# Router logits from rows before the first norm, the output product by halves, and another order of the last expert and the last norm

## The reference, cut to what matters

```python
def _finish(x, nsa_o, hg_o, ga, gb, w_pa, w_pb, w_o, ln1_g, ln1_b, moe_w, ln2_g, ln2_b):
    mix = (sigmoid(ga) * (nsa_o @ w_pa) + sigmoid(gb) * (hg_o @ w_pb)) @ w_o
    h = _layernorm(DN_ALPHA * x + mix, ln1_g, ln1_b)
    return _layernorm(DN_ALPHA * h + _moe(h, *moe_w), ln2_g, ln2_b)

def _moe(x, w_router, b_router, w_gu, b_gu, w_dn, b_dn):
    logits = x @ w_router + b_router
    top_v, top_e = top_k(logits, 4); gate = softmax(top_v)
    # for each of the 32 experts e, over the rows that chose it:
    h = xb @ w_gu[e] + b_gu[e]
    gt = minimum(h[:, :D_FF], 7.0); up = clip(h[:, D_FF:], -7.0, 7.0)
    ys = ((up + 1.0) * (gt * sigmoid(1.702 * gt))) @ w_dn[e] + b_dn[e]
    # y = the sum over a row's four experts of gate * ys
```

## Time and profile before

| | |
|---|---|
| Time, median of 3 runs | 1409.96 us (1408.92 to 1412.66) |
| Profiled execution, time / span | 1412.07 us / 1410.4 us |
| TensorE busy | 1378.1 us, 98% of the span |
| VectorE, ScalarE, GpSimd busy | 436.0, 296.8, 93.2 us |
| DMA moved | 476.70 MB, 464.85 MB of it through SP's queue |
| TensorE's granted clock, mean | 0.993 of full |

### The profile page before, as it was taken

One profiled execution on the slowest core, in us unless ns is written; L12 is line 12 of the kernel. 1 busy time (PEld: TensorE's weight loads), 2 busy tenths in 40 slices (PEclk: granted clock), 3 DMA queues, 4 the chain that ended last, 5 costly groups with the idle time before them and its releaser, 6 DMA issues.

```text
span 1410.4 us, 20548 instructions
## 1 busy us (share of the span) xinstructions
PE 1378.1 (98%) x7829; PEld 656.6 (47%) x7829; DVE 436.0 (31%) x946; ACT 296.8 (21%) x507; POOL 93.2 (7%) x122
## 2 busy tenths in 40 slices
PE   9999999998999999999999999999999999999996
PEld 6667999766774433333333333333333333333332
DVE  0345774763335321122112211221113111221115
ACT  1125531342311311111111111111112111111111
POOL 0031400203000000000000000000000000000000
PEclk9999999999999999999999999999999999999998
DMA  8831350729784999999999999999999999999993
GB/s 293 285 106 57 109 165 23 211 80 293 210 310 197 404 372 425 428 428 426 428 429 428 428 428 428 428 428 429 428 428 429 428 428 428 428 429 429 427 430 129
DMA packets 77622, 476.70 MB, mean 338 GB/s; under 512 B 9506, under 2 KB 37474, under 8 KB 52674
## 3 DMA queue, kind: packets, MB, share of 16 engines
q1 hardware_dynamic: 73328, 464.85, 81.3%
q0 software_dynamic: 2288, 9.51, 2.0%
q10 hardware_dynamic: 1954, 1.63, 0.4%
HBM read 471.54 MB, written 8.59 MB: 340 GB/s over the span
## 4 chain that ended last, share of the span: by engine, by line
PE 86%; DMA 10%; DVE 2%; ACT 1%; issue 0%; SPq 0%
PE bank L1313 27%; PE bank L1346 14%; DMA big<-in_w_gu 9%; PE bank L1003 4%; PE bank L1277 4%; PE bank L1256 4%; PE bank L765 3%; PE bank L749 2%; PE bank L1172 2%; PE bank L820 2%; PE bank L822 2%; PE bank L828 2%; PE bank L1185 2%; PE bank L1249 2%; PE bank L1267 1%; PE bank L1335 1%
## 5 line engine op out<-in xcount | busy, mean ns | idle before, releaser
L1313 PE MATMUL bank<-big,gates 128*64 128x512 f32 x1536 | 338.4, 594 | 4.5 <-DMA big<-in_w_gu 4.2
L1313 PEld LDWEIGHTS bank<-big,gates 128*64 128x64 f32 x1536 | 107.2, 137 | 216.7 <-issue 204.2
L1346 PE MATMUL bank<-big,gates 128*64 128x512 f32 x768 | 171.4, 595 | 0.0
L2397 DVE TENSOR_SCALAR gates<-bank 128x512 f32<-128x512 f32 x32 | 22.1, 692 | 434.5 <-PE bank L1326 434.5
L1653 ACT ACTIVATE gates<-gates 128x512 f32<-128x512 f32 x32 | 20.1, 630 | 452.1 <-DVE gates L2397 452.1
L1346 PEld LDWEIGHTS bank<-big,gates 128*64 128x64 f32 x768 | 53.0, 137 | 114.1 <-issue 114.1
L1727 POOL TENSOR_TENSOR gates<-gates,nsaT 128x192 f32<-128x192 f32 x64 | 31.4, 511 | 983.3 <-PE bank L1356 860.4
L2420 DVE TENSOR_TENSOR work<-work,bank 128x512 f32<-128x512 f32 x128 | 82.1, 682 | 42.5 <-PE bank L1277 42.5
L2416 DVE TENSOR_TENSOR work<-work,bank 128x256 f32<-128x256 f32 x32 | 13.5, 421 | 202.2 <-PE bank L1280 202.2
L1277 PE MATMUL bank<-gates 64*128 64x512 f32 x260 | 73.4, 641 | 0.9 <-ACT gates L1663 0.9
L1661 ACT ACTIVATE gates<-bank 128x512 f32<-128x512 f32 x32 | 19.1, 597 | 258.4 <-PE bank L1280 258.4
(11 more groups left out here) (391 smaller groups left out, 1622.0 us busy)
## 6 DMA issues: line engine op xcount, KB each, us to landing
big<-in_w_gu SPq DMA_DIRECT2D x96, 2048.0 KB, 22.7
big<-in_w_dn SPq DMA_DIRECT2D x48, 2048.0 KB, 25.9
front_rows<-in_w_gu SPq DMA_DIRECT2D x16, 2048.0 KB, 23.3
front_cols<-in_w_gu SPq DMA_DIRECT2D x15, 2048.0 KB, 21.5
front_cols<-in_w_dn SPq DMA_DIRECT2D x8, 2048.0 KB, 26.1
front_rows<-in_w_dn SPq DMA_DIRECT2D x8, 2048.0 KB, 28.6
big<-in_w_in SPq DMA_DIRECT2D x5, 2048.0 KB, 8.6
big<-in_cache_cmp_kv SPq DMA_DIRECT2D x64, 128.0 KB, 2.6
```

What stands on the lines that cost most here:

```text
L1313: last = pe.matmul(psum[2 + n][half * CAP:(half + 1) * CAP, :], xe[:, k % 4, (k // 4) * CAP:(k // 4 + 1) * CAP], weights_gu(slot, k % 2, c ...
L1346: last = pe.matmul(psum[5][half * CAP:(half + 1) * CAP, :], act_T[:, k % 4, (k // 4) * CAP:(k // 4 + 1) * CAP], ring_dn[slot][:, k % 4, ha ...
```

## The change

It does this:

1. Gate weights 3 go to another place in `big`, in two loads, and wait for the recurrence's states as well. The window rows of pass 0 no longer wait for products 7 and 8: two wait for four gate products, two for six. PE waits for all four at key block 8. Gate weights 4 are loaded as before and gate weights 5 after the eighth product.
2. `w_o` is stored and loaded as two halves of 512 columns, and `out_product` runs in the order 0, 2, 1, 3 (both first halves, then both second halves).
3. PE turns r = alpha*x + mix instead of h. The router's weights are multiplied by the norm's gain once (DVE), and each row's logits are scaled by its reciprocal deviation and moved by a multiple of the weights' sums afterwards. For this PE turns the gain and shift (16x128) and sums the scaled weights over partitions by a product with ones. h itself is scaled and shifted in six halves that stand between and behind the selections; the gather of expert 0 waits for them.
4. The loads of the expert weights ahead of expert 0 are put in another order. The gates' softmax is moved behind the count of rounds, POOL waits for it, and ACT copies alpha*h earlier.
5. The last expert is written out apart (PE and ACT) without gather and transposes for a next one. Its `combine` 1 and 2 and the transposes of the gates stand among the products with `w_dn`.
6. At the end the sample rows stay in quarters: statistics per quarter are joined by two products with a matrix of 0.25. The order is tile 0, sample rows, tile 1. Of tiles 0 and 1 the second half of the columns is scaled by ACT, and DVE multiplies by the gain and adds the shift.

```diff
-            sp.wait_ge(fill_done, 4)
+            sp.wait_ge(state_step, HH * 4)
+            sp.wait_ge(fill_done, 3)
             load_gates(3)
             load_rows(sp, 0, 3, rows_loaded[0])
-            for b4 in range(4):
+            for b4 in (2, 3, 0, 1):
                 if b4 % 2 == 0:
-                    sp.wait_ge(fill_done, 6 + b4)
-                if b4 == 2:
-                    sp.wait_ge(win_loaded, 32)
+                    sp.wait_ge(fill_done, 6 - b4)
                 load_window(0, b4, win_loaded)
             sp.wait_ge(pv_done, len(ITS))
             load_gates(4)
+            sp.wait_ge(fill_done, 8)
             load_gates(5)
...
                     if n == 8:
-                        pe.wait_ge(win_loaded, 32)
-                    if n == 10:
                         pe.wait_ge(win_loaded, 64)
...
             out_product(0)
+            pe.wait_ge(route_made, 11)
+            pe.matmul(psum[0][:, 2 * NE:4 * NE], C("ones"), wr_part, start=True, stop=True).then_inc(route_sent, 1)
+            turn_r(0)
+            turn_r(1)
+            out_product(2)
+            router_part(0, 0)
+            router_part(0, 1)
+            turn_r(2)
             out_product(1)
-            turn_h(0)
-            out_product(2)
-            pe.wait_ge(params_loaded, 32)
-            router_product(0)
-            out_product(3)
-            turn_h(1)
+            turn_r(3)
+            router_part(1, 0)
+            pe.wait_ge(route_made, 12)
+            out_product(3, {4: (lambda: turn_r(4),), 6: (lambda: router_part(1, 1),)})
+            router_part(2, 0)
+            turn_r(5)
             keep_busy(1)
-            router_product(1)
-            turn_h(2)
-            keep_busy(1)
-            router_product(2)
+            router_part(2, 1)
             keep_busy(4)
...
-            keep_busy(3)
+            keep_busy(4)
...
                 for k in range(KD):
+                    if k == 2 and final:
+                        combine(i, 1)
+                    if k == 3 and final:
+                        pe.wait_ge(y_added, i * 5 + 9)
+                    if k == 4 and final:
+                        combine(i, 2)
+                        turn_gates(i)
...
+            apply_half(1, 0, 3)
+            apply_half(1, 1, 5)
+            residual(1, 1, 5)
+            norm_scale(1, 2)
             select_tile(1)
+            scale_logits(2)
             select_tile(2)
             dve.wait_ge(select_ready, 3)
+            apply_half(2, 0, 4)
...
+            end_scale(0, 0)
+            end_apply(0).then_inc(own.next("end_step"), 1)
+            end_second(0).then_inc(y_ready, 1)
...
+            end_apply(1).then_inc(y_ready, 1)
+            end_second(1).then_inc(y_ready, 1)
```

More of the change, by code:

```diff
@@ L260, in trunk_kernel @@
         w_pb = part(big, 4096, [HH, D])
-        w_o = part(big, 8192, [KD, D])
+        w_o = [part(big, 8192 + 4096 * half, [KD, 512]) for half in range(2)]
         front_cols = sb("front_cols", [P, KD * NT + 2 * HG * NT])
@@ L338, in trunk_kernel @@
         b_router = part(small, 554, [NE])
+        wr_part = part(small, 256, [2 * NE])
+        wr_sums = part(small, 320, [2 * NE])
+        gb = part(small, 384, [2 * KD])
+        gb_rows = part(small, 426, [P])
+        ln_move = part(small, 586, [3])
+        wr_b = part(work, 6144, [KD, NE])
         ln_parts = part(small, 640, [3, 2, 6])
@@ L352, in trunk_kernel @@
         ln2 = [part(big, D * n, [D]) for n in range(2)]
+        ln2_q = [part(big, 2 * D + D // 4 * n, [D // 4]) for n in range(2)]
+        mean_of = part(nsa_flat, 1024, [P])
+        ln_sum = part(small, 690, [4])
+        ln_shift = part(small, 694, [2])
         xg = part(xT, 0, [512])
@@ L1184, in out_product @@
+            pe.transpose(psum[0][:, 0:2 * KD], gb_rows[0:2 * KD, :], ident[0:2 * KD, 0:2 * KD]).then_inc(route_sent, 1)
+            def out_product(i, between={}):
                 for k in range(KD):
[L1185 removed]
+                    for work_ in between.get(k, ()):
+                        work_()
+                    last = pe.matmul(psum[(5 + i) % 8][:, :], mixT[:, k, (i // 2) * P:(i // 2 + 1) * P], w_o[i % 2][:, k, :],
@@ L1283, in combine, with turn_gates, expert @@
                 last.then_inc(comb_done, 1)
-            def expert(group, q):
+            def turn_gates(i):
+                pe.wait_ge(pg_ready, i + 1)
+                for t in range(3):
+                    last = pe.transpose(psum[0][:, t * P:(t + 1) * P], pg[:, t, :, :].rearrange("p a n -> p (a n)"), ident)
+                last.then_inc(pg_turned, 1)
+            def expert(group, q, final=False):
                 i = group * 4 + q
@@ L1330, in expert @@
                 combine(i, 0)
-                gather(i + 1)
+                if not final:
+                    gather(i + 1)
                 pe.wait_ge(act_ready, i + 2)
@@ L1350, in expert @@
                         last.then_inc(piece_free, 1)
-                combine(i, 2)
-                pe.wait_ge(pg_ready, i + 1)
-                pe.wait_ge(xg_copied, i + 2)
-                for t in range(3):
-                    last = pe.transpose(psum[0][:, t * P:(t + 1) * P], pg[:, t, :, :].rearrange("p a n -> p (a n)"), ident)
-                last.then_inc(pg_turned, 1)
+                if not final:
+                    combine(i, 2)
+                    pe.wait_ge(xg_copied, i + 2)
+                    turn_gates(i)
             gather_sample(0)
@@ new lines, in _ @@
+            dve.wait_ge(r_ready, 6)
+            for half in range(2):
+                norm_stats(h_rows, 2, half)
+            norm_scale(2, 0)
+            residual(0, 0, 2)
+            dve.wait_ge(route_sent, 4)
+            step(dve.tensor_copy(wr_sums, psum[0][:, 2 * NE:4 * NE]))
+            dve.tensor_tensor(wr_sums[:, NE:2 * NE], wr_sums[:, NE:2 * NE], b_router, ALU.add).then_inc(route_made, 1)
+            dve.wait_ge(route_made, 12)
+            scale_logits(0)
+            apply_half(0, 0, 1)
```

365 lines of the change are left out of this document (241 added, 124 removed).

## The result

| | before | after |
|---|---|---|
| Time, median (range) | 1409.88 us (1407.82 to 1412.66), 12 runs | 1411.32 us (1408.78 to 1413.93), 12 runs |
| Profiled execution, time / span | 1412.07 / 1410.4 us | 1411.22 / 1409.5 us |
| Ratio of times | | 1.0016, 95% interval 1.0009 to 1.0023 |

The change makes the kernel slower by 0.16%, about 2 us: within the 0.3% that the prediction counts as no change, but on the other side of it than the forecast of 1406.5 us, and just above its range of 1402.0 to 1411.0.

A forecast was written before the change was run, and what follows sets the result against it. The prediction took the end to hang on expert 0's start, through PE freeing ring places for weight loads. Terms -4.87, +0.6 and -0.2 gave -4.5 us; between 1407.6 and 1405.5 it took 1406.5 us, range 1402 to 1411.

The forecast's parts named there:

- part 1: Window rows and gate weights, pass 0: PE's 2.13 us wait and the half clock behind it go, -4.87 us.
- rival A: New PE gaps ahead of the count and in the last expert bring half clock, 1.7 us each: 1409.9 us; chance 0.21.
- What bounds the kernel: Experts: their end hangs on when PE frees ring places early on, so expert 0's start moves the end equally.
- nothing within the later experts does: Later experts: no change within them moves the experts' end; no time was reckoned there.
- part 3: Last expert: products with `w_dn` end later, less follows them, so the end's first product starts 1.2 us later.
- Rival B: Pass 1: the window's wait moves to POOL's selected rows, making the kernel slower, 1414.5 us; chance 0.07.
- Part 2: Router, up to expert 0: output product ends 4.5 us later, DVE's chain takes 7.2 us; +0.6 us in all.
- Part 4: The end: DVE's work from the last results to the last store shrinks by 1.4 us.
- C: Router, last expert and end: chains shorter than reckoned, -3 instead of +0.4 us, 1403.1 us; chance 0.22.
- D: Ahead of expert 0: its start doesn't move, as a weight piece or small load comes last; 1409.7 us; chance 0.05.

The follow-up runs named there:

- b1: The kernel before, unchanged, profiled again: 1408.77 us.
- e4: The changed kernel with the last expert back in the loop but the new end kept: 1406.78 us, ratio 0.9983 to before.
- e9: e4 with ACT's alpha*h copy earlier, router products of 128 columns for prompt rows only, and three more keep_busy products: 1405.37 us, ratio 0.9972 to before.
- e6: The changed kernel with four products nobody reads in PE's two gaps in the last expert: 1409.42 us, ratio 0.9999 to before.
- e2: The kernel before with only PE's last four experts written out behind the loop: 1410.18 us, ratio 1.0006.
- e5: e4 with PE's last four experts written out behind the loop, in the loop's own order: 1408.35 us, ratio 0.9996 to before.
- e3: The changed kernel with the last expert and the end as before: 1408.62 us, ratio 0.9993 to before.
- e1: The kernel before with only the gate-weight and window-row changes: 1409.33 us, ratio 0.9995.
- e8: e1 with router products of 128 columns instead of 32, for all rows: 1408.00 us, ratio 0.9991 to before.
- e10: e8 with the sample rows' router products of 32 columns again: 1406.57 us, ratio 0.9977 to before.
- b2: The kernel before, unchanged, profiled once more: 1408.66 us.

## Why the prediction was wrong, point by point

Start from b1, which is what ordinary faster executions of before look like, and go to the changed kernel's profile: G 0.15 earlier, G to O 1.8 less, O to E 2.5 more, E to L 1.0 more, L to end 0.9 more; together +2.5 us. The forecast had -4.87 for G to O, +0.6 for O to E, nothing for E to L and -0.2 for L to end, together -4.5. So the four stretches came out 3.1, 1.9, 1.0 and 1.1 us longer than forecast: the term of part 1 was more than twice too large, rival A's half clock came at both its places, and late code, which no rival had, lengthened the stream.

- **What bounds the kernel: right up to its last clause.** Places free up, loads leave and the hole ends 3.3 us earlier, as expert 0 does, and no experiment moved E to L by more than 0.5 us but the late code. That exception is what the last clause, "nothing within the later experts does", had ruled out (see part 3).
- **Part 1, -4.87 us: the wait went as forecast, the size was wrong, the largest error.** The step that failed is the 2.7 us of half clock in the sum, taken from one execution as if each had it. At full clock G to O shrinks by 1.8 us (b1 to after), which is about b1's wait of 1.94. The other 2.9 (G to O of the first profile less b1's) were the half clock of the one execution that was profiled. I had written that faster executions might have less of it, and took 1.0 us off the gain for it (1406.5 against 1405.5 us), too little. The page "TensorE: Matmul & The Clock Gate" of the Trainium skill (section "Why this matters for your kernels"), by whose bound the part was worth the wait only, came nearer the typical time, though its bound for a gap does not describe, where half clock does follow 2.13 us. Rival B didn't come: POOL's rows stayed without a wait.
- **Part 2, +0.6 us: near at full clock (b1 to e4: 47.70 to 48.56, +0.86), with luck, and +2.5 in the changed kernel's profile.** DVE's chain took 7.0 us against my 7.2, but the last output half is ready only 3.2 us later behind O and not 4.5, so that the count comes 0.6 us earlier behind O (40.24 to 39.62) where I had +0.1. From the count to expert 0 it is 1.5 us more (7.46 to 8.94), where I had 0.5 for `keep_busy`: there stands a wait that I did not see. DVE's start needs ACT's last copy, put behind two copies that wait for PE, and it costs PE 1.05 us (1.30 against 0.25 in e9). The two errors nearly cancel. The other 1.64 us in the changed kernel's profile are half clock behind the 2.03 us ahead of the count, which I had named in rival A and priced at 1.7.
- **Part 3, +1.2 us: the order right, the step incomplete.** At full clock (e6) `combine` starts 20.18 us behind L, before 19.08: +1.1. The changed kernel has 21.81, 1.6 more for half clock, the other half of rival A. What I had in no rival is the code: writing the last group out makes PE load it again while the chain hangs on the weights, +1.2 us in E to L of e2 (against the mean of before's three profiles) and +1.56 of e5 (against e4). The step that failed is "nothing within the later experts does": in E to L I had put the written-out code at nothing, and it took 1.0 to 1.6 us.
- **Part 4, -1.4 us: right, and a little small.** DVE's last stretch is 1.9 us shorter. L to end falls by 1.6 from e3 to e4, since 0.2 are given back by a product that now stands ahead of the first `combine`.
- **Rivals.** A is what the profile shows, at both its places and its prices; with 0.21 it was too low, for PE's gaps of 1.8 to 2.0 us were nearly as long as the one in rows 4. That it came ahead of the count in the execution profiled is partly chance, as e4's full clock behind the same gap shows. C, that everything is shorter, was too high. D did not come.

The Trainium skill ("Runtime: NRT & Kernel Launch", "Instruction fetch mechanics") says that code comes in 16 KiB blocks by a DMA queue of the engine's own, which agrees with the 16 KB transfers here, and that crossing into the next block is mostly hidden. No wait of PE is put down to it in these traces; what it costs, it costs the weights' transfers, in the part that then lands last.

What stays open: why e1's executions split in two. The router comes 2 to 3 us earlier there and has half clock for 10.2 us or, by its times, hardly any; e8 and e10 show that more columns there end it, not what sets it off. Nor is it shown what decides, behind the same gap of PE, between full and half clock.

## What to carry to other kernels

Before pricing a stretch at half clock, see whether other executions have it: their mean granted clocks against their times tell, and the wait alone is the safe part of the sum. Where the end hangs on a stream of weights, count everything that shares its DMA engines, loading of code too; a loop that is written out in such a stretch brings transfers of code, and a part of each weight piece that falls behind by one was late to the end here. Where an edit removes work beside a wait of PE, put products nobody reads in its place first, and then measure what the edit is worth.

## What the runs showed of the hardware

- Half clock came in stretches of 3.4, 6.8 and 10.2 us. The kernel before had two of them, 10.2 us together, between G and the last product in one trace and none in two others. A PE wait of 1.94 us was followed by none (b1), one of 2.12 by none (b2), one of 2.13 by 6.8 us. A gap of 2.02 us ahead of the count was followed by none (e4) and by 3.4 us (e3).
- 16 KB code transfers of 1.0 to 1.2 us each during a full stream of weights put single parts of every later piece back by some 1.5 us, and the last part by 0.9 to 1.5: 898.65 to 899.16 us from expert 0 to the last piece without, 900.15 to 900.39 with it, in ten traces and in four.
- Sixteen fp32 products with 128x128 weights take 1.97 us with 32 columns (b1) and 2.05 with 128 (e8); with 128x32 weights 0.69 (e1) and 1.94 us (e8).
